# Loading each expert weight matrix in two transfers with 4096-byte rows, in a two-layer mixture-of-experts backbone

## What is computed

```python
N_EXPERTS, TOP_K, D_MODEL, D_EXPERT, MOE_BLOCK = 64, 8, 1024, 256, 128

def expert_block(args):                 # one block: 128 token slots of one expert
    tok, e = args
    xb = h_pad[tok]                     # 128 x 1024, gathered
    return (jax.nn.silu(xb @ w_eg[e]) * (xb @ w_eu[e])) @ w_ed[e]

y = lax.map(expert_block, (row_tok.reshape(n_blocks, MOE_BLOCK), block_e)).reshape(n_rows, D)
routed = jnp.zeros((T + 1, D), h.dtype).at[row_tok].add(y * row_w[:, None])[:T]
```

## Time and profile before

| what | value |
|---|---|
| time, median of 3 runs (lowest, highest) | 3413.23 us (3405.48, 3416.39) |
| time of the profiled execution, and its span | 3434.55 us, 3432.8 us |
| PE busy | 3124.5 us (91%) |
| DVE, ACT, POOL busy | 51%, 40%, 19% |
| TensorE's mean granted clock | 0.97 |
| moved by the DMA engines | 703.53 MB, mean 205 GB/s |
| expert weight transfers | 141 x 3 of 1024 KB |

### The profile page before, as it was taken

One profiled execution on the slowest core, in us unless ns is written; L12 is line 12 of the kernel. 1 busy time (PEld: TensorE's weight loads), 2 busy tenths in 40 slices (PEclk: granted clock), 3 DMA queues, 4 the chain that ended last, 5 costly groups with the idle time before them and its releaser, 6 DMA issues.

```text
span 3432.8 us, 48887 instructions
## 1 busy us (share of the span) xinstructions
PE 3124.5 (91%) x14864; PEld 2225.6 (65%) x14864; DVE 1748.8 (51%) x2560; ACT 1369.8 (40%) x1977; POOL 643.7 (19%) x767
## 2 busy tenths in 40 slices
PE   6999999999997999999999499999998799999994
PEld 3468877899644766666666346776764576666663
DVE  1354371222363766666666426362324476666665
ACT  2253261221223555555555335252212455555552
POOL 0000310000061222222222200020004222222222
PEclk9999999999999999999999799999999899999997
DMA  6320113333318999999999510113332999999993
GB/s 235 113 86 7 53 42 107 129 129 135 126 52 310 347 353 346 349 352 359 350 356 310 172 51 1 34 38 92 92 126 86 336 353 341 340 353 342 333 329 131
DMA packets 223714, 703.53 MB, mean 205 GB/s; under 512 B 55651, under 2 KB 104197, under 8 KB 169429
## 3 DMA queue, kind: packets, MB, share of 16 engines
q1 hardware_dynamic: 176356, 601.80, 46.9%
q0 software_dynamic: 47248, 100.21, 11.5%
HBM read 669.89 MB, written 98.31 MB: 224 GB/s over the span
## 4 chain that ended last, share of the span: by engine, by line
PE 63%; DMA 23%; issue 5%; DVE 4%; ACT 2%; SPq 2%; POOLq 0%; POOL 0%; ACTq 0%; DVEq 0%
DMA region_v<-in_w_exp_up 10%; DMA ring<-in_w_exp_up 8%; PE ps L825 7%; PE ps L906 6%; PE ps L832 6%; PE ps L833 6%; PE ps L834 6%; PE ps L854 5%; DMA region_k<-in_w_exp_up 4%; PE ps L1104 4%; PE ps L877 4%; PE ps L879 4%; PE ps L878 4%; PE ps L1009 3%; PE ps L1030 3%
## 5 line engine op out<-in xcount | busy, mean ns | idle before, releaser
L877 PE MATMUL ps<-region_h_split,region_q_split 128*128 128x512 f32 x846 | 348.8, 412 | 84.5 <-DVE ring_split L1534 35.6
L1954 POOL DMA_INDIRECT acc<-region_q,idx_out x141 | 226.5, 1606 | 970.7 <-DVE region_q L1567 856.8
L854 PEld LDWEIGHTS ps<-con,region_c 128*128 128x128 f32 x1686 | 225.7, 167 | 109.8 <-issue 80.8
L834 PE MATMUL ps<-region_x_split,ring_split 128*128 128x384 f32 (+2 forms) x800 | 285.1, 356 | 0.0
L1194 ACT ACTIVATE region_h<-ps 128x256 f32<-128x256 f32 x141 | 54.4, 386 | 553.7 <-PE ps L879 515.2
L1534 DVE TENSOR_TENSOR ring_split<-ring,region_h_split 128x1024 fp32r<-128x1024 f32 x210 | 244.5, 1220 | 38.7 <-ACT region_h_split L1171 38.6
L854 PE MATMUL ps<-con,region_c 128*128 128x128 f32 x1686 | 252.6, 278 | 7.7 <-issue 2.2
L906 PE MATMUL ps<-ring,region_c 128*128 128x512 f32 x560 | 252.0, 593 | 1.0 <-DVE region_c L1546 1.0
L877 PEld LDWEIGHTS ps<-region_h_split,region_q_split 128*128 128x128 f32 x846 | 160.0, 189 | 134.9 <-DVE ring_split L1534 44.6
L1171 ACT ACTIVATE region_h_split<-ring 128x1024 fp32r<-128x1024 f32 x210 | 206.7, 1049 | 46.6 <-DMA ring<-in_w_exp_up 46.4
L878 PE MATMUL ps<-ring_split,region_q_split 128*128 128x512 f32 x560 | 218.8, 391 | 0.0
(11 more groups left out here) (315 smaller groups left out, 6822.0 us busy)
## 6 DMA issues: line engine op xcount, KB each, us to landing
ring<-in_w_exp_gate SPq DMA_DIRECT2D x70, 1024.0 KB
ring<-in_w_exp_up SPq DMA_DIRECT2D x70, 1024.0 KB
ring<-in_w_exp_down SPq DMA_DIRECT2D x70, 1024.0 KB
ring<-in_w_mod SPq DMA_DIRECT2D x24, 2048.0 KB, 8.0
region_k<-in_w_exp_gate SPq DMA_DIRECT2D x36, 1024.0 KB
region_k<-in_w_exp_up SPq DMA_DIRECT2D x36, 1024.0 KB
region_k<-in_w_exp_down SPq DMA_DIRECT2D x36, 1024.0 KB
region_v<-in_w_exp_gate SPq DMA_DIRECT2D x35, 1024.0 KB
```

Source lines behind the costliest of these rows:

```text
L834: last = mm(o, wl, xh, start=False, stop=k == len(stationary) - 1)
L854: last = nc.tensor.transpose(ps[0:t.shape[1], at:at + t.shape[0]], t, ident[0:t.shape[0], 0:t.shape[0]])
L877: mm(m_gu[s], xT_hi[s][:, k, :], high, start=k == 0, stop=False)
L1954: pool.indirect_dma_start(ACC[s], bass.IndirectOffsetOnAxis(ap=idx_out[:, s:s + 1], axis=0), yb[:, s, :], None, bounds_check=TOK - 1, oob_ ...
```

## The change

Each 1 MiB matrix is loaded in two transfers. For gate and up, the first one brings the first half of each partition's eight rows of 256 numbers, the second one the other half; for down, the first brings the first of each partition's two rows of 1024 numbers, the second the second. In each transfer a partition gets 4096 bytes, at a pitch of 8192 bytes in memory. All transfers of a slot's gate and up still add to one semaphore, and its users wait for all of them: the counts double. Nothing else changes.

```diff
                 def load_gate_up(e, s):
                     for g, w in enumerate((w_exp_gate, w_exp_up)):
-                        sp.dma_start(wgu[s][:, g, :, :].rearrange("p k n -> p (k n)"),
-                                     w[l][bass.ds(e, 1), :, :].rearrange("e (p k) n -> (e p) (k n)", p=P))\
-                            .then_inc(sl[f"wgu{s}"], 16)
+                        rows = w[l][bass.ds(e, 1), :, :].rearrange("e (p k) n -> (e p) k n", p=P)
+                        for ks in (slice(0, DK // 2), slice(DK // 2, DK)):
+                            sp.dma_start(wgu[s][:, g, ks, :].rearrange("p k n -> p (k n)"),
+                                         rows[:, ks, :].rearrange("p k n -> p (k n)")).then_inc(sl[f"wgu{s}"], 16)
 
                 def load_down(e, s):
-                    sp.dma_start(wdn[s].rearrange("p c n -> p (c n)"),
-                                 w_exp_down[l][bass.ds(e, 1), :, :].rearrange("e (p c) n -> (e p) (c n)", p=P))\
-                        .then_inc(sl[f"wdn{s}"], 16)
+                    rows = w_exp_down[l][bass.ds(e, 1), :, :].rearrange("e (p c) n -> (e p) c n", p=P)
+                    for cc in range(2):
+                        sp.dma_start(wdn[s][:, cc, :], rows[:, cc, :]).then_inc(sl[f"wdn{s}"], 16)
...
-                                pe.wait_ge(sl[f"wdn{before}"], 16 * (m + 1))
+                                pe.wait_ge(sl[f"wdn{before}"], 32 * (m + 1))
...
-                    act.wait_ge(sl[f"wgu{w}"], 32 * turns)
+                    act.wait_ge(sl[f"wgu{w}"], 64 * turns)
...
-                        act.wait_ge(L[l]["wgu0"], 32)
+                        act.wait_ge(L[l]["wgu0"], 64)
```

## The result

The changed kernel takes 3443.48 us (median of 4 runs, 3442.48 to 3443.52) against 3414.3 us for the kernel before in the same comparison: a ratio of 1.009, 95% interval 1.0072 to 1.0108. It is slower by 29 us; forecast were +33.

What follows compares the result with a forecast made beforehand. The prediction took weight transfers to pace both expert loops; 0.26 us more for each block gave 19.5 us in layer 0 plus 13.3 in layer 1, +33 us on the median of 3413.2, so 3446 us, range 3412 to 3475.

Steps and rivals of the forecast that it cites:

- What bounds the kernel: Both expert loops: a block's time is its transfers' time, in layer 0 clearly, in layer 1 by little; TensorE's floor 10.13 us.
- The sum: Both loops: 19.5 us in layer 0 plus 13.3 in layer 1, together +33 us, to 3446 us, +1.0%.
- The four fifths for layer 1: Layer 1's loop: only 13.3 of 16.6 us counted, since DMA engines idle 5% and its work is near TensorE's.
- the ends: Both loops: lower +0.16 us a block from x and ctx loads, upper +0.37 from w_out; 3431 to 3465 us.
- Rows of 4096 bytes in place of 8192: Weight loads in both loops: 408 GB/s in place of 422, 7.71 us against 7.45, 0.26 us more for each block.
- Six issues in place of three: SyncE's queue in the loops: about 1.3 us more issuing for each block, in idle time; some issues of some microseconds; nothing counted.
- idle time absorbs it: Rival, both loops: idle time takes up the cost, leaving nothing to 10 us, about 3417 us; chance 0.18.
- finer rows mix better: Rival, loops: shorter rows mix better with gathers, up to -0.3 us a block, -42 us, 3371 us; chance 0.12.
- The last rival: Loops: surcharge for each row, or skipped half costs; 76 us (3489) if half is paid again, 114 (3527) if all; chance 0.12.
- What would show it: Profile after: lower loop rate, weights alone about 408 GB/s, 11.3 and about 10.95 us a block, same chain, some long issues.
- The early stretch: Early in layer 0, TensorE sets the pace at 10.13 us a block on loads issued ahead; it was to end sooner.
- The prediction's sign for the pitch: Weights moving alone: a rate under 400 GB/s would show that skipping every other 4096 bytes costs.

Runs made afterwards that it cites:

- runs without down loads: Kernel before and changed kernel, each loading down for the first four blocks only and reusing it: 3339.71 us (8192-byte rows) and 3336.75 us (4096), loops 1411 us in both.
- contiguous halves: Changed kernel, but each of a matrix's two transfers takes 512 KB lying together in memory, tokens transposed to match: ratio 1.0014 to the kernel before, loops 1488 us.
- The tiny transfers: Kernel before plus three transfers for each block, each 16 rows of 8 bytes, weights keeping 8192-byte rows: 3423.18 us, ratio 1.0024, loops 1496 us.
- two thirds of the change: Kernel before with only gate and up split at a pitch as in the change, down still in one transfer: 3462.24 us, ratio 1.0144, loops 1536 us.
- two pairs of kernels: All rows 4096 against gate and up 4096 with down 8192: loops 1488 and 1507 us with transfers together in memory, 1517 and 1536 at a pitch.

## Why the prediction was right, point by point

**What bounds the kernel** was right. The loops are paced by their transfers, and the runs without down loads show it from the other side: with TensorE in front, splitting gate and up costs nothing.

**The sum** was right in size: +33 us against 29 in the medians and 31 in the loops. That it came so close is luck, as the next point shows. Layer 0 was put at 19.5 and measured 15, layer 1 at 13.3 and measured 16. The four fifths for layer 1 were not borne out: its idle 5% took up nothing of this cost. (With the ends, 76 x 0.16 and half of 65 x 0.16 are 17.4 us, not 18.)

**The step "Rows of 4096 bytes in place of 8192" was near in its number and wrong in its cause.** It took 408 GB/s from 512 KB loads with the same row length and count of completions, as if nothing else had held them. But these loads are issued from 3397 us on and are slow at first, with the engines busy all the same, and the window of the earlier trace rows takes in the end of that: its first microsecond moves at 320 GB/s, and from 3401 to 3408 us the same loads run at 420:

```profile
DMA packets 88, 0.32 MB, mean 320 GB/s; under 512 B 10, under 2 KB 10, under 8 KB 88
...
DMA packets 808, 2.94 MB, mean 420 GB/s; under 512 B 90, under 2 KB 90, under 8 KB 808
```

Weights in contiguous halves move alone at 415 GB/s (1041 to 1051 us of that kernel), which is 7.58 us for a block, +0.13 and not +0.26; the pitched ones at 413 over 13 us. And in the loops contiguous rows cost 2 us in all.

The step set the place in memory aside as something "neither shows", with w_out's 402 GB/s as an upper end. That is where the other 29 us are: they come with the order in which the rows are taken, every other 4096 bytes in the changed kernel, or in turn from two places 512 KB apart where both halves travel in one transfer. They cost only while gathers and sums run beside them: alone, 413 and 415 GB/s hardly differ. Why the order matters is not settled. The engine time for each row is 174.4 ns at a pitch (0.751 x 16 x 650 / 44773) and 172.6 together, 0.09 us for each block of the 0.2 needed. As the kernel with both halves in one transfer costs the same 29 us, it is not the second pass over the same 8192 bytes.

**Six issues in place of three**: harmless, and issues were held, as forecast, though more of them and for longer than "some". The tiny transfers bound transfers, issues and completions together at 8 to 10 us, the contiguous halves at 2 us in the loops.

**The rivals.** That idle time absorbs it was given 0.18 and is what happens to the row length itself. That finer rows mix better holds in part: the gathers' queue needs 25.1% for 41.84 MB with contiguous halves, against 25.8% for 41.64 MB before. It is far too little to turn the sign. The last rival named the skipped half, and that is nearest to the cause, but at 76 us or more; the measured 0.2 us for each block is under even the 0.28 that it put on top of the row. That mixed lengths cost 19 us no rival had.

**What would show it.** The lower rate in the loops (2% under 352), the chain and the long issues came as written. 11.3 and 10.95 us for each block were forecast, 11.17 and 10.98 found. The early stretch ended sooner: in layer 0 nine distances between down products are 10.17 us, where before there were twelve of 10.13 to 10.17. The 408 GB/s for weights alone did not come, but 413 to 421. The prediction's sign for the pitch, a rate alone under 400, did not come either, though the order of the rows is the cause: it shows only beside other traffic.

## What to carry to other kernels

In a loop that its transfers pace, the order in which a load walks through memory can cost as much as one would put down to shorter rows or more transfers. Where a matrix must be split, split it so that each piece lies together, and arrange the other operand to match; by itself that gained nothing here over one transfer with long rows (1.0014). Don't split only some of the streams of a saturated queue before measuring it; here two thirds of the change cost more than the whole. And when a price is borrowed from another transfer with the same length, look first at whether the window has its start in it, and then make the runs that keep the length and change the rest, since the sum can agree while the cause is another.

## What the runs showed of the hardware

- Two transfers of 64 partitions in place of one of 128, rows of 8192 bytes: 513 ns for a row in place of 334, and 19% on the whole kernel.
- Rows of 4096 bytes at a pitch of 8192, or taken in turn from two places 512 KB apart, against the same rows lying together: 1517 and 1515 us for both loops against 1488. Alone, 413 against 415 GB/s.
- Rows of 4096 and 8192 bytes in one queue, in transfers of 512 KB and 1 MiB: 19 us over 141 blocks in two pairs of kernels.
- Rows of 4096 bytes in transfers of 512 KB, each in one piece, move alone at 415 to 420 GB/s once they run, rows of 8192 in 1 MiB at 422.
- Two SP issues in a row took 6.89 us in the changed kernel where single ones had taken 0.33 to 0.38 before; with contiguous halves such holding cost nothing.
- Whole spans of this kernel differ by some 20 us outside the loops between executions and chips, while the sum of both loops repeated within 1 us in the two profiles of the kernel before.
